# A two-layer hybrid block on one core: delta rule in chunks of 128 tokens instead of 64, row sums partly on VectorE, data laid out by feature on the host

## The reference, cut to what matters

```python
decay = jnp.exp(jnp.where(tril, gc[..., :, None] - gc[..., None, :], -jnp.inf))
kk = jnp.einsum('nbhid,nbhjd->nbhij', kc, kc)
m_low = jnp.where(strict, bc[..., :, None] * kk * decay, 0.0)
sol = lax.linalg.triangular_solve(m_low + jnp.eye(cs, dtype=f32), rhs, left_side=True, lower=True, unit_diagonal=True)
u, w = sol[..., :dv], sol[..., dv:]
...
    v_new = u_i - jnp.einsum('bhcd,bhde->bhce', w_i, state)
    o_i = jnp.einsum('bhcd,bhde->bhce', q_i * jnp.exp(g_i)[..., None], state) + jnp.einsum('bhij,bhje->bhie', qk_i, v_new)
    state = state * jnp.exp(g_last)[..., None, None] + jnp.einsum('bhcd,bhce->bhde', k_i * jnp.exp(g_last[..., None] - g_i)[..., None], v_new)
```

## Time and profile before

| | |
|---|---|
| median of 3 runs (lowest, highest) | 2139.86 us (2137.26, 2143.52) |
| the profiled execution | 2144.36 us, span 2142.3 us |
| mean granted clock of TensorE | 0.982 |
| busy: PE, PEld, DVE, ACT, POOL | 2042.4, 1539.8, 1121.6, 750.7, 0.2 us |
| data moved | 270.43 MB, mean 126 GB/s |

### The profile page before, as it was taken

The page is one execution under the profiler, slowest core; times in us unless marked ns, Lnnn a source line. Parts: engine busy times, 40 slices in busy tenths (PEclk is TensorE's granted clock), DMA queues, the critical chain, the costliest instruction groups (busy, mean ns, idle before and its releaser), DMA issues.

```text
span 2142.3 us, 28196 instructions
## 1 busy us (share of the span) xinstructions
PE 2042.4 (95%) x11503; PEld 1539.8 (72%) x11503; DVE 1121.6 (52%) x2062; ACT 750.7 (35%) x1547; POOL 0.2 (0%) x4
## 2 busy tenths in 40 slices
PE   6889999999999999999999899989999999999996
PEld 3247777777777777777777578767777777777875
DVE  1247575765757657476675432354555545554232
ACT  2443242332424224242333322263443433443231
POOL 0000000000000000000000000000000000000000
PEclk9999999999999999999999899999999999999998
DMA  8884334343333433434342144423122122213232
GB/s 307 330 318 158 129 126 139 118 137 129 128 121 126 148 118 118 148 108 138 118 144 83 40 138 146 143 84 103 60 84 76 67 79 84 80 40 128 98 110 96
DMA packets 59764, 270.43 MB, mean 126 GB/s; under 512 B 7411, under 2 KB 7797, under 8 KB 41589
## 3 DMA queue, kind: packets, MB, share of 16 engines
q1 hardware_dynamic: 59636, 268.64, 36.3%
HBM read 255.51 MB, written 13.11 MB: 125 GB/s over the span
## 4 chain that ended last, share of the span: by engine, by line
PE 84%; DVE 6%; ACT 4%; DMA 3%; issue 2%; SPq 1%; DVEq 0%; ACTq 0%
PE psum L549 23%; PE psum L551 20%; PE psum L550 20%; PE psum L679 3%; DMA ada_p<-in_ada_first 2%; PE psum L918 2%; PE psum L946 1%; PE psum L590 1%; DVE ada_acc L1407 1%; DVE w_lo L1370 1%; PE psum L930 1%; PE psum L729 1%; PE psum L738 1%; PE psum L765 1%; PE psum L783 1%
## 5 line engine op out<-in xcount | busy, mean ns | idle before, releaser
L549 PE MATMUL psum<-mov_hi,w_hi 128*128 128x512 f32 x2128 | 892.2, 419 | 32.4 <-DVE mov_lo L1420 11.3
L551 PE MATMUL psum<-mov_hi,w_lo 128*128 128x512 f32 x2128 | 838.2, 394 | 0.0
L550 PE MATMUL psum<-mov_lo,w_hi 128*128 128x512 f32 x2128 | 836.1, 393 | 0.0
L549 PEld LDWEIGHTS psum<-mov_hi,w_hi 128*128 128x128 f32 x2128 | 402.3, 189 | 170.8 <-issue 72.2
L551 PEld LDWEIGHTS psum<-mov_hi,w_lo 128*128 128x128 f32 x2128 | 402.3, 189 | 90.1
L1370 DVE TENSOR_TENSOR w_lo<-w_raw,w_hi 128x512 fp32r<-128x512 f32 x532 | 354.9, 686 | 206.7 <-ACT w_hi L1033 205.2
L550 PEld LDWEIGHTS psum<-mov_lo,w_hi 128*128 128x128 f32 x2128 | 403.8, 190 | 80.6 <-issue 8.6
L1033 ACT ACTIVATE w_hi<-w_raw 128x512 fp32r<-128x512 f32 x532 | 308.6, 620 | 5.1 <-DMA w_raw<-in_w_pack 5.1
L1407 DVE SCALAR_TENSOR_TENSOR ada_acc<-ada_t,silu_c,ada_acc 128x512 f32<-128x512 f32 x240 | 177.8, 741 | 1.4 <-DMA ada_t<-in_ada_late 0.5
L1730 DVE SCALAR_TENSOR_TENSOR res<-psum,mod,xr 128x512 f32<-128x512 f32 x32 | 24.0, 750 | 207.2 <-PE psum L551 207.2
L1258 ACT ACTIVATE osq<-res 128x512 f32<-128x512 f32 x32 | 20.2, 632 | 262.6 <-DVE res L1730 262.6
(11 more groups left out here) (272 smaller groups left out, 1820.5 us busy)
## 6 DMA issues: line engine op xcount, KB each, us to landing
w_raw<-in_w_pack SPq DMA_DIRECT2D x133, 1024.0 KB, 5.7
ada_t<-in_ada_late SPq DMA_DIRECT2D x128, 512.0 KB, 3.5
x_in<-in_ada_first SPq DMA_DIRECT2D x32, 512.0 KB, 8.1
ada_t<-in_ada_first SPq DMA_DIRECT2D x16, 512.0 KB, 9.0
ada_p<-in_ada_first SPq DMA_DIRECT2D x16, 512.0 KB, 9.0
xr<-x_spill SPq DMA_DIRECT2D x32, 256.0 KB, 2.7
x_in<-in_x SPq DMA_DIRECT2D x4, 1024.0 KB, 6.2
x_spill<-res SPq DMA_DIRECT2D x1, 4096.0 KB, 18.4
```

The lines of the kernel that those rows point to most:

```text
L549: mm(PJ[r], w_hi[r][:, ks], mov_hi[:, kt], start=(j == 0), stop=False)
L550: mm(PJ[r], w_hi[r][:, ks], mov_lo[:, kt], start=False, stop=False)
L551: ins = mm(PJ[r], w_lo[r][:, ks], mov_hi[:, kt], start=False, stop=(j == KC - 1))
```

## The change

- The delta rule runs in 4 chunks of 128 tokens. `kk_products` makes full 128x128 products. The diagonal 64x64 blocks of the triangular matrix are inverted as before; the corner block below the diagonal comes from two more products, `across_y` (with a copy, `across_copy`) and `across_z`, and VectorE's `across` puts it into `XT2`. The last `inverse_z` also updates the not turned inverse of the first block. `solve_u`, `solve_w`, `scan_a`, `scan_b` use whole 128x128 operands, and there are 4 scan steps (`SCAN`) instead of 8. `decay_exponents`, `decays` and `kk_decay` work on 128-wide rows. Gate sums start in the middle of a chunk, and `first_sum` is added as a bias in ScalarE's exponential (four instructions).
- `dec` and `XT2` share `pa[0]`; `CT`, `MT`, `Y` share `AT`; `MO` shares `tmpQ`. Waits for the former users are added.
- Slots move: `solve_*` from 54 to 58, the scan to 60, 62, then 0, 2, 3, 5, 6, 8 of the next head; `DA_S`, `DA_T` to (0, 5, 8, 12), (5, 8, 12, 17); `rule_sums` from 20 to 21; `ada_stage(h, 0)` from 31 to 32 behind `inverse_first`; `v_tokens` from 47 to 48.
- Output chunks: VectorE adds the squares into `ada_acc` (`add_square`), and TensorE makes two products by ones at the end of a layer (`row_sums`). ScalarE loads one table set ahead of the chunks.
- The host gives x by feature (`x_t`) and all small parameters packed. The start has no transposes, loads x straight into `res`, and the copy of x to `x_spill` (4 MB) is dropped; layer 0's output chunks read x itself.
- The output is stored by feature, and the host turns it. The transposes of the last chunks (`final_turn`) and their copies go. The last norm is 11 multiplies of 128x512 on VectorE and 5 on GpSimd, stored in 12 transfers.

```diff
+        CT, MT = [AT[:, a:a + 4 * CS].rearrange("p (t c) -> p t c", t=4) for a in (0, 4 * CS)]
+        Y = AT[:, 8 * CS:12 * CS]
+        dec = pa[0][:].rearrange("p (t c) -> p t c", t=4)
+        XT2 = dec
+        MO = tmpQ[:, 0:4 * CS].rearrange("p (t c) -> p t c", t=4)
...
-        DA_S, DA_T = (0, 4, 8, 13), (4, 8, 13, 17)
+        DA_S, DA_T = (0, 5, 8, 12), (5, 8, 12, 17)
+        SCAN = ((60, 62), (64, 66), (67, 69), (70, 72))
...
-            sp.dma_start(sums[:], t["consts2"]).then_inc(in_const, 16)
-            sp.dma_start(dtb[:], t["ev_dt_bias"].partition_broadcast(P)).then_inc(in_const, 16)
...
+                for kk in (2 * q - 2, 2 * q - 1):
+                    first_ada(0, kk)
+                sp.dma_start(res[:, q * 4 * T:(q + 1) * 4 * T], t["x_t"][q]).then_inc(in_x[q], 16)
+            for kk in (6, 7):
                 first_ada(0, kk)
...
-                        sp.dma_start(x_spill.rearrange("k p t -> p k t"), res[:].rearrange("p (k t) -> p k t", k=KC))\
-                            .then_inc(spilled, 16)
...
+            def store(a, b):
+                sp.dma_start(t["out"][a * P:b * P, :].rearrange("(k p) t -> p k t", p=P),
+                             res[:, a * T:b * T].rearrange("p (k t) -> p k t", t=T)).then_inc(stored, 16)
...
             def kk_products(h):
                 pe.wait_ge(qkn_ok, h * 2 + 2)
                 for i in range(TT):
-                    for r in range(2):
-                        c = slice(i * P + 64 * r, i * P + 64 * r + 64)
-                        mm(SA0[R[r], 64 * i:64 * i + 64], ck[:, c], ck[:, c], start=True, stop=True)
+                    mm(SA0[:, i * P:i * P + P], ck[:, i * P:i * P + P], ck[:, i * P:i * P + P], start=True, stop=True)
                 for i in range(TT):
-                    for r in range(2):
-                        c = slice(i * P + 64 * r, i * P + 64 * r + 64)
-                        ins = mm(SA0[R[r], 256 + 64 * i:256 + 64 * i + 64], ck[:, c], cq[:, c], start=True, stop=True)
...
+                else:
+                    for i in range(TT):
+                        c = slice(64 * i, 64 * i + 64)
+                        mm(SA1[R[0], c], XX[R[0], 1, c], Y[R[0], c], start=True, stop=True)
...
+            def across_y(h):
...
+                for i in range(TT):
+                    c = slice(64 * i, 64 * i + 64)
+                    ins = mm(SA0[R[1], c], MO[R[0], i, :], XX[R[0], 0, c], start=True, stop=True)
+                ins.then_inc(off_ok[0], 1)
...
+            def across_z(h):
...
+                for i in range(TT):
+                    c = slice(64 * i, 64 * i + 64)
+                    ins = mm(SA1[R[0], c], Y[R[1], c], XX[R[1], 1, c], start=True, stop=True)
+                ins.then_inc(off_ok[2], 1)
...
-                pe.wait_ge(yev_ok[5], h + 1)
                 for i in range(TT):
-                    for r in range(2):
-                        ins = mm(SA0[R[r], i * P:i * P + P], XX[R[r], 1, 64 * i:64 * i + 64],
-                                 cv[R[r], i * P:i * P + P], start=True, stop=True)
+                    ins = mm(SA0[:, i * P:i * P + P], XT2[:, i, :], cv[:, i * P:i * P + P], start=True, stop=True)
...
-                        ins = mm(dst[:, 64 * i:64 * i + 64], ck[R[r], i * P:i * P + P],
-                                 XX[R[r], 1, 64 * i:64 * i + 64], start=True, stop=True)
-                    ins.then_inc(W_ok, 1)
+                for i in range(TT):
...
             def scan_a(h, c):
...
+                pe.wait_ge(S_ok, h * 4 + c + 1)
+                mm(GW[:, 0:P], WT[:, c, :], S[:], start=True, stop=True).then_inc(ws_ok, 1)
 
...
             def scan_b(h, c):
...
-                ins = mm(GO[:, cc], vnew[R[r], :], qkd[R[r], i, :], start=False, stop=True)
-                if c < 7:
-                    ins = mm(GW[:, P:2 * P], kd[R[r], i * P:i * P + P], vnew[R[r], :], start=True, stop=True)
+                ins = mm(GO[:, cc], vnew[:], qkd[:, c, :], start=False, stop=True)
+                if c < TT - 1:
+                    ins = mm(GW[:, P:2 * P], kd[:, cc], vnew[:], start=True, stop=True)
                 ins.then_inc(so_ok, 1)
...
-                    st.setdefault(3 * (c - 2), []).append(lambda c=c: scan_a(h, c))
-                    st.setdefault(3 * (c - 2) + 2, []).append(lambda c=c: scan_b(h, c))
+                for c in range(1, TT):
...
+                      I0: [lambda: inverse_first(h), lambda: ada_stage(h, 0)], 48: [lambda: v_tokens(h)],
+                      I0 + 22: [lambda: across_y(h)], I0 + 24: [lambda: across_z(h)],
+                      58: [lambda: solve_u(h), lambda: solve_w(h)],
+                      SCAN[0][0]: [lambda: scan_a(h, 0), lambda: av_tokens(h)], SCAN[0][1]: [lambda: scan_b(h, 0)],
+                      63: [lambda: ada_stage(h, 1)]}
...
+            def row_sums(stage, osq_):
+
+                pe.wait_ge(acc_ok, (KC - 2) * (stage + 1))
+                mm(TR, ones, ada_acc[:], start=True, stop=False)
+                pe.wait_ge(osq_ok, KC * (stage + 1))
+                mm(TR, ones, osq_[1][:], start=False, stop=True).then_inc(oss_ok, 1)
...
-                        pe.wait_ge(osq_ok, i * 2 + (base + c))
-                        mm(TR, ones, osq_[(c + 1) % 2][:], start=(first and c == 1), stop=False).then_inc(oss_ok, 1)
...
-            def final_turn(k2, r):
...
-                for i in range(TT):
-                    ins = nc.tensor.transpose((OA, GO)[r][:, i * P:i * P + P], scaled[r][:, i * P:i * P + P], ident)
-                ins.then_inc(ftr_ok, 1)
...
             def decays(h):
                 act.wait_ge(dT_ok, h + 1)
-                f(dec[:], dec[:], ACT.Exp).then_inc(dec_ok, 1)
-                f(gB[:], GW, ACT.Exp).then_inc(egc_ok, 1)
+                f(pa[0][:], pa[0][:], ACT.Exp).then_inc(dec_ok, 1)
+                for i in range(TT):
+                    ins = f(gB[:, i * P:i * P + P], GW[:, i * P:i * P + P], ACT.Exp, bias=first_sum[:, i, h:h + 1])
+                ins.then_inc(egc_ok, 1)
...
+            def across_copy(h):
+                act.wait_ge(off_ok[0], h + 1)
+                f(Y[R[1], :], SA0[R[1], 0:256], ACT.Copy).then_inc(off_ok[1], 1)
...
+                f(WT[:], tile4(SA1), ACT.Copy).then_inc(wt_ok, 1)
 
...
+            nc.scalar.preload_act_table_set("natural_log_exp_and_others")
...
+            nc.scalar.preload_act_table_set("natural_log_exp_and_others")
...
-            f(xr2[0][0:1, :], xr2[0][0:1, :], ACT.Exp, scale=-0.5).then_inc(frow_ok, 1)
+            act.wait_ge(oss_ok, 2)
+            step(f(rs2[0][:], TR, ACT.Ln, scale=1.0 / D, bias=EPS))
+            f(GO, rs2[0][:], ACT.Exp, scale=-0.5).then_inc(frs_ok[0], 1)
+            f(rs2[1][:], rs2[0][:], ACT.Exp, scale=-0.5).then_inc(frs_ok[1], 1)
...
+                wait(dve, at_ok, h * 4)
+                step(V.tensor_tensor(dec, tile4(GW), head_col(gc, h).to_broadcast([P, 4, P]), ALU.subtract))
+                V.tensor_tensor(dec, dec, con("neg").unsqueeze(1).to_broadcast([P, 4, P]), ALU.add).then_inc(dT_ok, 1)
...
             def kk_decay(h):
...
+                wait(dve, pv_ok, h)
+                for r in range(2):
+                    c = slice(64 * r, 64 * r + 64)
+                    ins = V.tensor_tensor(MT[R[r]], tile4(SA0)[R[r], :, c], dec[R[r], :, c], ALU.mult)
+                step(ins)
+                V.tensor_tensor(MT, MT, head_col(beta, h).to_broadcast([P, 4, 64]), ALU.mult).then_inc(kk_out, 1)
+                V.tensor_tensor(qkd[:], tile4(SA1), dec, ALU.mult).then_inc(kk_out, 1)
+                step(V.tensor_tensor(MO[R[0]], tile4(SA0)[R[0], :, 64:128], dec[R[0], :, 64:128], ALU.mult))
+                V.tensor_tensor(MO[R[0]], MO[R[0]], head_col(beta, h)[R[0]].to_broadcast([64, 4, 64]), ALU.mult).then_inc(mo_ok, 1)
...
+                    V.tensor_tensor(CT, MT, lev(l + 1), ALU.mult).then_inc(ct_ok[l + 1], 1)
                 else:
-                    V.tensor_tensor(XT_, XT_, SA1[:, 256:512], ALU.subtract).then_inc(xfin_ok, 1)
+                    for r in range(2):
+                        V.tensor_tensor(XT2[R[r], :, 64 * r:64 * r + 64], tile4(XT_)[R[r]], tile4(SA1[R[r], 256:512]), ALU.subtract)
+                    V.tensor_tensor(XX[R[1], 1, :], XX[R[1], 1, :], SA1[R[1], 256:512], ALU.subtract)
+                    V.tensor_tensor(XX[R[0], 0, :], XX[R[0], 0, :], SA1[R[0], 0:256], ALU.subtract).then_inc(xfin_ok, 1)
+
+            def across(h):
+
+                V.memset(XT2[R[1], :, 0:64], 0.0)
+                dve.wait_ge(off_ok[2], h + 1)
+                V.tensor_scalar(XT2[R[0], :, 64:128], tile4(SA1[R[0], 0:256]), -1.0, None, ALU.mult).then_inc(off_ok[3], 1)
...
-                                       in1=bU[R[r], i * P:i * P + P], op0=ALU.mult, op1=ALU.add).then_inc(vn_ok, 1)
+                V.scalar_tensor_tensor(out=vnew[:], in0=GW[:, 0:P], scalar=nbeta[:, c, h:h + 1],
+                                       in1=bU[:, c * P:c * P + P], op0=ALU.mult, op1=ALU.add).then_inc(vn_ok, 1)
...
```

(10 more changed lines are left out.)

391 lines of the change are left out of this document (154 added, 237 removed).

## The result

The changed kernel takes 2070.09 us (median of 4 runs, 2067.24 to 2072.82) against 2140.57 (4 runs, 2137.26 to 2143.52): a ratio of 0.9671, 95% interval 0.9649 to 0.9693, so 70.5 us less.

| stretch | forecast | measured |
|---|---|---|
| start, to the first `inverse_first` (187.77 -> 172.21; the spill is in it) | -17 | -15.6 |
| seven periods of a head (918.1 -> 904.1) | -25 | -14.0 |
| tail of the last head, to the first output chunk | -8 | -8.5 |
| 15 distances between chunks, layer 0 | -11 | -13.4 |
| from there to the first output chunk of layer 1 | -2.6 | -4.0 |

The account below looks back on a forecast made before the run. TensorE issuing without a pause (84% of the chain) was taken as the bound; -16 - 1 - 33 - 11 - 2.6 - 17 - 3.4 = -84 us gave 2060 for a profiled-like execution, 2056 as median, range 2028 to 2084.

Parts of the forecast that it names:

- Contents of a head: TensorE's work in one head, from scan, solves, kk_products, across products and last inverse_z: -7.2 us a head.
- second rival: Full products keep the fixed part of 0.3 us and the waits come too: 2075 us; chance 0.12.
- (a): Slots 8 to 12 of a head: VectorE's list makes turn late by 1.3 us.
- (b): Slots 12 to 17 of a head: VectorE's list makes the next turn late by 1.5 us.
- (c): Slots 26 to 32 of a head: VectorE's longer kk_decay and decay_exponents make inverse_first late by 2.0 us.
- first rival: VectorE is not late in the heads, which then give 58 us: about 2031 us; chance 0.13.
- Per head -3.5, seven times -25: Steps between heads, VectorE's lateness included: 3.5 us less a head, 25 us less over seven.
- fourth rival: Three waits a head cool TensorE's clock, each losing 1.7 us, 36 in all: 2092 us; chance 0.06.
- Chunks: Output stages: without TensorE's sums, 0.85 us a chunk, -11 in layer 0; with transposes 1.28, -17 in layer 1.
- Start: Square-sum and modulation rounds of 2.0 us begin earlier and end at 47 us instead of 63: -16 us.
- third rival: Start is bound by transfers anyway, so x by feature gains a third of the 16 us: 2067; chance 0.08.
- Table loads: One set for logarithm and exponential removes two loads of 1.28 us at each layer's end: -2.6 after layer 0.

Follow-up runs that it names:

- e12: e11 with the start's squares summed on VectorE and the split of slot 15 moved behind combine in slot 16; 2015.7 us, ratio 0.9407.
- e1: Changed kernel with k_scaled and two MO multiplies (2.1 us) moved on VectorE from ahead of inverse_first to later; 2048.1 us, ratio 0.9562.
- e2: Changed kernel with VectorE's five modulation tiles moved from slots 8 to 16 to slots 18 to 22; 2061.8 us, ratio 0.9621.
- e3: Changed kernel with the edits of e1 and e2 together; 2030.2 us, ratio 0.9478.
- e5: Changed kernel with only the two MO multiplies (0.83 us) moved from ahead of inverse_first, k_scaled left in place; 2060.4 us, ratio 0.9622.
- e10: Changed kernel with ada_stage ahead of inverse_first in slot 32, not behind it; 2058.7 us, ratio 0.9606.
- e6: Changed kernel with both output stages' squares summed on TensorE again, one product with the ones per chunk; 2096.1 us, ratio 0.9785.
- e9: Changed kernel with the start's squares of x added on VectorE and one TensorE product instead of 16; 2066.3 us, ratio 0.9638.
- e8: Changed kernel without the two preloads of the logarithm and exponential table set ahead of the output stages; 2078.0 us, ratio 0.9703.
- e7: Changed kernel with the start's first four modulation rows copied ahead of the eight splits of the first weight chunks; 2069.3 us, ratio 0.9661.
- e11: Changed kernel with e1, e2 and e7 together, conv_silu of k moved to slot 16 and one table load at the start; 2026.8 us, ratio 0.9456.

## Why the prediction was right, and where it was short

**Contents of a head: right.** `scan_a` 0.25, `scan_b` 0.69, `solve` 1.8, and `across_y` and `across_z` 0.8 each were within 0.1 of their terms. A head of the changed kernel without a fall takes 128.0 us with 5.0 of waits, before it took 131.15 with 0.7: the contents saved 7.5 us, forecast 7.2. By e12's heads (122.7 with 0.2 of waits) it is 7.9. The working had a slip that brought it nearer by accident: eight chunks of 1.5 us, the last without its third product, are less than 12.0 and not 12.2. The full products keep a fixed part of 0.03 us at most and not 0.3, so the second rival is out.

**(a), (b), (c): right in place and nearly in size.** 1.09, 1.82, 1.91 against 1.3, 1.5, 2.0. e1 and e2 show that VectorE's list sets them: each went away with the work that was taken out, whole or by most. The first rival (VectorE not late, 2031) describes what the kernel would have been without them; e3, where 0.7 of the 4.8 us are left, is close to that kernel, at 2030.2.

**The term that was mis-sized is "Per head -3.5, seven times -25": it measured -14.0.** The heads in which the clock stayed up had 128.0 and not 127.6, 0.4 us or 3 in all; the prediction's own terms, -7.2 + 4.8 - 0.5, make -2.9 a head, its steps between heads -3.5, and such a head measured -3.2. The other 8 us are five falls of the clock of 1.6 us behind the wait of (c). The prediction had this as its fourth rival and argued against it with the length of the waits ("none of the three reaches the length of those gaps", in the tail of the last head). That step failed: e5 and e10 show falls behind waits of 1.1 and 1.04 us. The rival priced a fall of 1.7 us at each of three waits in seven heads, 36 us, and a fall did measure 1.6; but it took part at one of the three waits and not in every head, so the time came out between forecast and rival. The Trainium skill's rule that gaps in TensorE's work bring the clock down (TensorE: Matmul & The Clock Gate, HAM oscillation — how this bites in real kernels) holds here at one place of a head and, behind an equally long gap in slot 17, doesn't.

**Chunks: right, a little small, and then some luck.** 0.91 for 0.85 and 1.34 for 1.28 a chunk (e6 separates the 0.91). Both forecasts took 10.95 from slots of 1.37; the chunk without a sum is 10.88. Thirteen times this is 11.8 and 17.4 us; the other 1.6 and 1.5 us of the table lie in the first distances of a stage, and those are luck. The fifteen distances took 159.0 us (layer 0) and 156.2 (layer 1) in the profiled execution of the changed kernel, and 159.3 to 161.9 and 156.8 to 160.9 in the other runs whose sums are on VectorE.

**Start: the size right (-15.6 for -17), the reason incomplete.** Both the last square sum and the first `inverse_first` came 15 to 16 us earlier, as said. But the sum's chain of 2.0 us rounds is not what sets the time now. Before, the transfers ran at 293 GB/s from 10 to 80 us; after, at 412 from 10 to 50. Before, their queue stood there for 37.8 us until modulation products and for 13.3 us until the turning of x freed a buffer, and from 70 to 80 us it moved 149 GB/s, the hole of the rows that the changed kernel has too; which of these set the pace, no run separates. That stretch of the kernel before (columns as in the earlier trace rows):

```profile
10.00:80.00 70.00, 53.57 (x215) 20.99 (x214) 15.68 (x30) 29.80 (x49) 0.00 (x0) 0.93 0.81 293
```

e9 shows that shortening the chain alone is paid only as far as the transfers have a hole. The third rival (bound by transfers) had this mechanism and too small a gain for it.

**Table loads: right behind layer 0** (2.7 for 2.6, e8; the rest of that stretch's -4.0 lies within what it varies by, 540.6 to 543.6 us among the runs with the same code), and in the end's term one of two loads was hidden before too; the end gave 2.6 for 3.4.

**Open.** Which of two heads with the same wait and the same work keeps its clock, the runs don't settle. The same code of the heads gave 5, 6, 6, 7 and 7 falls in five profiled executions (changed kernel, e6, e9, e7, e8), and shorter heads (e2) gave 8. Why slot 32 and not slot 17 is also open. What differs in the rows is what follows the wait: in slot 32 `inverse_first` on quarters of the array and `ada_stage` with one column, in slots 12 and 17 `turn` with 128 columns on the whole array; no run varied that alone.

## What to carry to other kernels

When a change thins out the bounding engine's list, write down the list of the engine beside it slot by slot and ask of each item ahead of a handover who needs it, and when: here 2.1 us of work that stood ahead of slot 32 and was due at slot 48 or later cost 22 us of kernel, and moving it and five tiles gave 40 us on top of the change's 70. Price a wait of TensorE at more than its length; at the one sensitive place a wait of 1.0 to 2.7 us cost 0.7 to 2.3 us of clock on average on top (3 to 10 falls of 1.6 us behind seven waits). And when transfers run at their full rate through a stage, look for the hole in them before shortening the chain of products.

## What the runs showed of the hardware

- Behind a wait of TensorE of 1.03 to 2.67 us at one place of a head, the granted clock fell from 2.4 to 1.2 GHz for a short stretch, in steps that cost 1.6 us each, none, one or two of them. Counted behind the six waits that lie in seven periods: 2 falls with waits of 1.14 us, 4 with 1.04, 5 to 7 with 1.91 (8 in shorter heads), 8 with 2.65. Without the wait, in 28 periods of four runs (e1, e3, e11, e12), there were none.
- Waits of 1.09 and 1.82 us in slots 12 and 17 of the heads never lowered it (14 of them in e1, which has no fall in its heads).
- In e8 the next activation starts 0.02 us after the 1.28 us of a table load.
- GpSimd's multiply of 128x512, which had no row before, takes 1.23 us (6.16 for the five of them, starting at 2051.78 us; spans of GpSimd are rough), inside the forecast's bounds, and ends 7.5 us before the span does.
